# Three chained blocks on one core: large tiles moved to multiples of 128 bytes, and each 512-column projection product written as two of 256

## What is computed

```
hn = rms_norm(h, g); proj = hn @ w_in                 # layer 1, 2048 -> 7832 columns
o_a = nsa_mixer(q, k_cmp, v_cmp, k_slc, v_slc, k_win, v_win, gates, ...)
o_b = rwkv7_mixer(feat_b, ...)
h = h + rms_norm(concat(o_a * silu(z_a), o_b * silu(z_b)) @ w_out, g2)
x = x + (mla_attend(q, k, v) * silu(gate)) @ w_out    # layer 2, latent projections up and down
x = x + (rms_norm(diff_attend(...)) * silu(gate)) @ w_out   # layer 3, 2048 -> 8192 columns
```

## Time and profile before

| | |
|---|---|
| time, median of 3 runs | 3158.12 us (3154.66 to 3159.01) |
| the profiled execution, first to last instruction | 3154.7 us |
| mean granted TensorE clock | 0.998 |
| PE busy | 3118.6 us (99%), 21457 products |
| DVE, ACT, POOL busy | 1762.0, 1274.4, 193.0 us |
| 512-column projection products (L550 to L552, L566 to L568, L580 to L582) | 3 x (2864 + 64 + 160) = 9264 |
| 256-column products of `tokens` (L594 to L596) | 3 x 640 = 1920 |

### The profile page before, as it was taken

One profiled execution on the slowest core, in us unless ns is written; L12 is line 12 of the kernel. 1 busy time (PEld: TensorE's weight loads), 2 busy tenths in 40 slices (PEclk: granted clock), 3 DMA queues, 4 the chain that ended last, 5 costly groups with the idle time before them and its releaser, 6 DMA issues. The chain is left out here.

```text
span 3154.7 us, 51865 instructions
## 1 busy us (share of the span) xinstructions
PE 3118.6 (99%) x21457; PEld 2553.3 (81%) x21457; DVE 1762.0 (56%) x3081; ACT 1274.4 (40%) x2328; POOL 193.0 (6%) x154
## 2 busy tenths in 40 slices
PE   8999999999999999999999999999999999999999
PEld 6877777777878778788888888888888888888787
DVE  4335565565666744644457776335556655665822
ACT  4124333433444422523346665323344434443421
POOL 0000000001011101000001010110000000000000
PEclk9999999999999999999999999999999999999999
DMA  8433333332232353343332213534223323332452
GB/s 253 114 81 91 90 94 96 100 111 60 70 98 70 110 165 108 109 110 100 107 104 54 61 51 121 163 104 117 87 81 94 94 76 99 94 95 81 158 163 77
DMA packets 494639, 324.25 MB, mean 103 GB/s; under 512 B 27194, under 2 KB 449693, under 8 KB 494406
## 3 DMA queue, kind: packets, MB, share of 16 engines
q1 hardware_dynamic: 494374, 320.94, 34.9%
q10 hardware_dynamic: 32, 0.01, 0.0%
HBM read 276.05 MB, written 44.85 MB: 102 GB/s over the span
## 5 line engine op out<-in xcount | busy, mean ns | idle before, releaser
L538 DVE TENSOR_TENSOR WLT<-AR,WHT 128x1024 fp32r<-128x1024 f32 (+1 forms) x430 | 527.0, 1231 | 668.1 <-ACT WHT L532 667.7
L550 PE MATMUL PS<-XH,WHT 128*128 128x512 f32 (+1 forms) x2224 | 896.0, 403 | 3.7 <-issue 1.4
L552 PE MATMUL PS<-XH,WLT 128*128 128x512 f32 (+1 forms) x2224 | 872.0, 392 | 0.0
L532 ACT ACTIVATE WHT<-AR 128x1024 fp32r<-128x1024 f32 (+1 forms) x430 | 447.5, 1043 | 604.9 <-PE PS L552 475.0
L551 PE MATMUL PS<-XL,WHT 128*128 128x512 f32 (+1 forms) x1712 | 668.7, 391 | 0.0
L550 PEld LDWEIGHTS PS<-XH,WHT 128*128 128x128 f32 (+1 forms) x2224 | 416.7, 187 | 101.6 <-issue 9.5
L552 PEld LDWEIGHTS PS<-XH,WLT 128*128 128x128 f32 (+1 forms) x2224 | 416.9, 187 | 97.2
L551 PE MATMUL PS<-ARR,WHT 128*128 128x512 f32 x1024 | 404.6, 395 | 0.0
L551 PEld LDWEIGHTS PS<-XL,WHT 128*128 128x128 f32 (+1 forms) x1712 | 320.9, 187 | 71.0 <-issue 4.0
L551 PEld LDWEIGHTS PS<-ARR,WHT 128*128 128x128 f32 x1024 | 192.4, 188 | 40.3 <-issue 0.2
L550 PE MATMUL PS<-XL,WHT 128*128 128x512 f32 x512 | 203.3, 397 | 0.1
(11 more groups left out here) (511 smaller groups left out, 5197.8 us busy)
## 6 DMA issues: line engine op xcount, KB each, us to landing
AR<-b_w_in SPq DMA_DIRECT2D x128, 512.0 KB, 4.0
AR<-w_in SPq DMA_DIRECT2D x122, 512.0 KB, 4.0
AR<-a_w_in SPq DMA_DIRECT2D x48, 512.0 KB, 4.5
AR<-w_out SPq DMA_DIRECT2D x32, 512.0 KB, 4.2
AR<-a_w_out SPq DMA_DIRECT2D x32, 512.0 KB, 4.0
AR<-b_w_out SPq DMA_DIRECT2D x32, 512.0 KB, 4.1
proj_scratch<-AR SPq DMA_DIRECT2D x33, 256.0 KB, 2.1
residual_scratch<-RES SPq DMA_DIRECT2D x8, 1024.0 KB, 5.4
```

Of the source, the lines that this page charges most:

```text
L532: self.nc.scalar.activation(self.shaped(self.high, n), self.shaped(self.raw, n), ACT.Copy).then_inc(self.s_high, 1)
L538: self.nc.vector.tensor_tensor(self.shaped(self.low, n), self.shaped(self.raw, n), f32(self.shaped(self.high, n)), ALU.subtract).then_inc( ...
L550: mm(out, wh, xh[k0 + c], start=(start and c == 0), stop=False)
L552: last = mm(out, wl, xh[k0 + c], start=False, stop=(stop and c == nk - 1))
```

## The change

Three edits.

First, addresses. `aligned` now asserts a multiple of 128; `fill_line` puts padding where needed (24 floats behind `C`, none at the head), and `ARENA` grows by 24 floats to a multiple of 32 floats. `PRM`, `STG`, `AR`, `ARR` move up by 96 bytes, and `EXT`, `ONESR`, `WHT`, `WLT` by 192; all of them, and `RES`, `XH`, `XL`, `C` as before, then start at a multiple of 128 bytes.

Second, order inside the arena: in `nsa` the tile `W2` is taken before the small tiles, in the recurrence the stretch of `3 * (T + 1)` is rounded up and the small tiles `WC2` and `OMK` are taken last, so that large tiles there start at multiples of 128 bytes too.

Third, `matmuls`, `pair` and `features` issue each product through `halved`: columns 0 to 255, then 256 to 511, into the two halves of the same bank, with the same weights. `tokens` is not touched in its instructions. The weights are named in each MATMUL, and each has its own LDWEIGHTS in the trace.

```diff
+HT = T // 2
-ARENA = 17064
+ARENA = 17088
+LINE = 128
...
 def aligned(nc):
-    return (nc.sbuf_base + 31) // 32 * 32
+    base = (nc.sbuf_base + 31) // 32 * 32
+    assert base % LINE == 0, base
+    return base
...
         self.C = self.sb("C", [P, nconst])
+        self.fill_line("PAD_C")
...
+    def fill_line(self, name):
+
+        gap = -((self.nc.sbuf_base + 31) // 32 * 32) % LINE
+        if gap:
+            self.sb(name, [P, gap // 4])
...
+    def halved(self, out, w, x, start, stop):
+
+        self.nc.tensor.matmul(out[:, 0:HT], w, x[:, 0:HT], start=start, stop=False)
+        return self.nc.tensor.matmul(out[:, HT:T], w, x[:, HT:T], start=False, stop=stop)
...
-        mm = self.nc.tensor.matmul
+        mm = self.halved
...
-    n = 3 * (T + 1)
-    return flat[:, 0:n], flat[:, n:n + P], flat[:, n + P:n + P + T + 1]
+    n, m = 3 * (T + 1), lines(3 * (T + 1))
+    return flat[:, 0:n], flat[:, m:m + P], flat[:, m + P:m + P + T + 1]
...
-    VC, KCT = room.take(NKV * HD), room.take(NKV * NCMP)
+    VC = room.take(NKV * HD)
+    W2 = room.tiles(2, P)
+    KCT = room.take(NKV * NCMP)
...
-    take(3 * (T + 1))
+    take(lines(3 * (T + 1)))
...
-    WC2 = [take(NCH) for _ in range(2)]
...
-    OMK = take(NPAIR)
     QT, Y = take(T), take(T)
     EV = room.tiles(2)
+    OMK = take(NPAIR)
+    WC2 = [take(NCH) for _ in range(2)]
```

More of the change, by code:

```diff
@@ L169, in __init__ @@
         cc, nconst = const_cols()
+        self.fill_line("PAD_HEAD")
         at = [aligned(nc)]
@@ L654, in first_pair_inputs, with lines @@
     flat = k.RES[:, :, :].rearrange("p a t -> p (a t)")
-    n = 3 * (T + 1)
-    return flat[:, 0:n], flat[:, n:n + P], flat[:, n + P:n + P + T + 1]
+    n, m = 3 * (T + 1), lines(3 * (T + 1))
+    return flat[:, 0:n], flat[:, m:m + P], flat[:, m + P:m + P + T + 1]
+def lines(n):
+    return (n + LINE // 4 - 1) // (LINE // 4) * (LINE // 4)
 def nsa(k, st, tiles, ntile, res_out):
@@ L682, in nsa @@
     TAB = room.take(NH)[0:NBUCKET + 1, :]
-    W2 = room.tiles(2, P)
     OH = E.rearrange("p h m -> p (h m)")[0:NBUCKET + 1, 0:T + P]
```

## The result

The changed kernel takes 3218.39 us (median of 4 runs, 3216.67 to 3224.42), the kernel before 3157.93 us beside it. The ratio is 1.0203, with a 95% interval of 1.0191 to 1.0216: 2% slower, where 1% faster was forecast, and 8 us above the upper end of the range.

The account below looks back on a forecast made before the run. PE was taken as the bound. Aligned triples (12.4 us), `ARR` triples (13.2) and `tokens` of layer 3 (6.8) take 32.4 off the 3154.7 us span; adding 3.4 for the median gives 3126 us, range 3096 to 3210.

Parts of the forecast that it names:

- What bounds the kernel: Whole kernel: PE, busy 99% of the span, bounds it; the distance between PE's products sets the time.
- The pace of a half, 113.5 ns: Split products: each 256-column half takes 113.5 ns, a triple 681.0 ns, as the fast 256-column products of `tokens` do.
- the two kinds of triples: Groups of three products: 2064 with both parts aligned, 12.4 us less; 1024 with `ARR`, 13.2 us less.
- Loads: Weight loads on PE: about 0.10 us per 128 x 128, fitting under a half of 107 ns.
- Alignment as a gain: Products with `ARR`, 32 bytes off a multiple of 128: aligning it gives back 6.9 ns a triple, over 1024 triples.
- `tokens` of layer 3, -6.8 us: Instructions unchanged, `ARR` and weights become aligned: 512 triples go from 353.7 to 340.5 ns, 6.8 us less.
- Instruction fetch, nothing: Fetching queue: 18528 more instructions, 1.0 MB more, cost nothing because fetching lies beside PE's work.
- The range: Whole kernel: 3096 to 3210 us, from half a nanosecond or more gained per half up to the slow end.
- the slow pace: Rival: halves run at 117.7 ns everywhere, giving 3203 to 3210 us; chance 0.22.
- point of decision, 115.1 ns: 256-column products: from this pace on, 20064 of them take what the same work takes now, 2128.5 + 181.1 us.
- The fixed price per instruction: Rival for split products: one more instruction costs 2.7 ns, a pair 231.7 ns; +11 us, 3169; chance 0.10.
- The rule on SBUF lines: Operand addresses: by 16-byte lines alignment gives nothing, making the sum 14 us smaller, about 3140 us.

Follow-up runs that it names:

- split_w64: The changed kernel with 64 bytes of padding ahead of WHT and WLT, split kept: 3194.24 us, ratio 1.0125 to the kernel before.
- split384: The changed kernel with the cut moved from column 256 to 384: 3662.78 us, ratio 1.1607 to the kernel before.
- split320: The changed kernel with the cut moved from column 256 to 320: 3413.97 us in its one run.
- same256: The changed kernel with products whole and 128 bytes of padding ahead of the arena: 3134.02 us, ratio 0.9934 to the kernel before.
- align_only: The changed kernel with the split taken back and all addresses kept: 3162.4 us, ratio 1.0027 to the kernel before.
- split_only: The kernel before with `halved` and nothing else, its addresses kept: 3201.83 us, ratio 1.0149 to the kernel before.

## Why the prediction was wrong

- *What bounds the kernel*: right. PE had 99% before and after, and every result of the study is the sum of distances between its products.
- *The pace of a half, 113.5 ns*: this is the step that failed. It gave -25.6 us for the two kinds of triples; the trace after gives +62.0. The pace was read from `tokens`, where activations are stationary and the weights lie 64 bytes over a multiple of 128, and the reason for taking it, that an aligned stationary operand brings it, was never tried. The change itself took the weights from 64 to 0, and there no stretch of halves has the fast pace and `tokens` lost it. Nor is 64 enough: `split_w64` has weights and activations where `tokens` of layer 3 runs at 113.4 to 113.7, and 14 of its 173 stretches of halves with XH/XL or RESR are fast, the others at 117.1 to 117.8. Why a stretch takes one pace or the other is open. The measured pace of the change is 118.7 with XH/XL (134 stretches) and 118.2 with ARR: (2 x 118.7 - 229.1) x 6192 + (2 x 118.2 - 231.35) x 3072 = 51.4 + 15.5 = 67 us, against 62 in the table; the products at the ends of a stretch, which cost about the same either way, make up the rest.
- *Loads*: "a load thus fits under a half of 107 ns, with little to spare" is wrong. The 0.10 us came from eight distances of which the first was short, 28 ns; the other seven are 112 ns, and `split384` and `split320` show 108 to 112 ns as the time that a product must give its successor. A half of 106.7 ns falls 1 to 5 ns short of it. That sets the price of the uneven cuts, but of what the change lost it explains a part at most: halves at 113.3 and at 118 ns have the same loads. Two loads are 216 to 224 ns, under the 229.0 of a whole product, and the fastest halves seen, 226.7 a pair, would have been a small gain over before. They would not have been one over `same256`, where whole products reach 226.8 to 227.3 without the split.
- *Alignment as a gain*: half wrong. The -7 us for ARR came (231.6 against 239.5 us in `align_only`), but 192 bytes more under the weights cost 16 us on XH/XL, a loss that was given no term. Multiples of 128 are no rule here; what was taken from the earlier trace rows as "off by 32 bytes" was one point of a pattern in 256.
- *`tokens` of layer 3, -6.8 us*: nothing came (118.3 against 117.9 to 119.1), since the weights went to 0, not 64. In layer 2 the fast pace was lost: 47.1 us for 45.5.
- *Instruction fetch, nothing*: right, 1.2 MB more (1.0 was estimated) and no wait.
- *The range*: its lower end does not follow from its own sum, 26 us under 3126 being 3100 and not 3096; the miss was at the other end.
- *The rivals*: the slow pace, at 0.22, is what happened. Its mechanism was stated only as a pace; its price of 117.7 ns was 0.5 to 1 ns short, and so 3210 lay 8 us under the result. Its point of decision, 115.1 ns, fits all four kernels that are cut at 256: all are slower than before, with most stretches above it. The fixed price per instruction is refuted by `split384`: the rule from which it was taken (the Trainium skill, TensorE: Matmul & The Clock Gate, Back-to-back issue gap) had the sign right and the size, 2.5 ns per split against 8, wrong. That section gives the formula for an isolated product, and says that in a stream of loads and products both set the spacing; the uneven cuts agree with that. The same page, under LDWEIGHTS (loading the stationary operand), gives a load as its columns over 1.2 GHz, 107 ns for 128, which is just the length of a half; the traces have mostly 108 or 109 behind a short product in `split384` and `split320`, and 112 with one moving column.
- *The rule on SBUF lines* (the Trainium skill, SBUF — State Buffer, Specifications): by 16-byte lines all these places are alike. The runs differ by up to 6 ns a product among places that are all multiples of 32 bytes, so the measurement decides against using it that way.

## What to carry to other kernels

A product that is shorter than the load of the weights for the next one waits for it, here 0.11 us for 128 x 128 of 4-byte weights, slightly more than 256 float32r columns at 2.4 GHz; cutting a product below that buys a wait, and the more unevenly it is cut the longer the wait. Where the load just about fits, at 256, this case shows no gain from the cut and no way to choose the pace. Price a product by the distance between starts in a stretch of the same role, stationary and moving operands not exchanged. When PE is the bound and products stand at some 229 ns for 213 ns of columns, the place of the weights against the activations within 256 bytes is worth a sweep, one padding at a time: the same instructions took from 226.8 to 233.4 ns here, and the best placement made the kernel 0.7% faster.

## What was not expected of the hardware

- The pace of a product beside a load goes with where both operands lie modulo 256 bytes, from 13.5 to 20 ns over the columns' own 213.3. For whole products the same place was best; for halves it was the worst of the three places tried (119.9 ns), and for the products of `tokens` weights at 64 with activations at 128 and ARR at 0 (113.4 to 113.7 ns). Whether the period is 256 or more was not tried, since no padding above 192 bytes was run, and why the place counts is open.
- The same instructions at the same addresses can run at two steady paces, a stretch at a time. The pace holds for a whole stretch and comes in a few values, 113.5, 115.5, 118 and 119 ns for halves in `split_only`. A stretch of halves at 113.3 ns and one at 117.8 have the same kinds of operands, shapes and places. The work beside them does not tell them apart either: in `split_w64` the fast ones run with the DMA engines busy for 73% (58 to 79 us) and for none (1691.2 to 1693.5 us) of the time, the slow ones likewise (all of it from 107 to 117 us, none from 93 to 103 us). What selects it stays open.
